# Four token blocks by fetched rows and six dense in the expert stage, with the low parts of u made by VectorE

## The reference, cut to what matters

```python
def peer(x, w_q, sub_keys, u, v):
    q = (xb @ w_q).reshape(tb, PEER_HEADS, 2, PEER_D_KEY // 2)
    s = jnp.einsum("thmd,mkd->thmk", q, sub_keys)
    s_top, i_top = lax.top_k(s, K)                    # K = 16, 8 heads
    ...
    best, pos = lax.top_k(cand, K)
    expert = jnp.take_along_axis(cand_idx, pos, axis=-1)
    gate = jax.nn.softmax(best, axis=-1)
    h = jax.nn.gelu(jnp.einsum("thkd,td->thk", u[expert], xb))
    w = gate * h
    return jnp.einsum("thk,thkd->td", w, v[expert])
```

## Time and profile before

| | us |
|---|---|
| median of 3 runs | 5527.01 (5522.74 to 5529.78) |
| span of the profiled execution | 5520.1 |
| experts stage in it (from its first load) | 3009.75 to 5520.1 |
| spread_gates in it, stores of the 7 blocks issued | 2752.8 to 2978.2 |

### The profile page before, as it was taken

The page is one execution under the profiler, slowest core; times in us unless marked ns, Lnnn a source line. Parts: engine busy times, 40 slices in busy tenths (PEclk is TensorE's granted clock), DMA queues, the critical chain, the costliest instruction groups (busy, mean ns, idle before and its releaser), DMA issues. The chain is left out here.

```text
span 5520.1 us, 71031 instructions
## 1 busy us (share of the span) xinstructions
PE 4860.9 (88%) x24196; PEld 3924.5 (71%) x24196; DVE 3732.9 (68%) x7021; ACT 1582.4 (29%) x2809; POOL 2631.3 (48%) x1877
## 2 busy tenths in 40 slices
PE   7999995554999799765396999999999999999999
PEld 6888884443444486554285788888888888888888
DVE  2000003786578422889896888888888888888887
ACT  3111101554667421111396222222222221222221
POOL 4122210553345110344574666666666666666664
PEclk9999997777899899887698999999999999999999
DMA  3222211001311342000187777677777767677676
GB/s 128 85 85 85 83 50 61 28 25 50 132 50 57 119 145 87 30 33 20 38 230 242 282 241 247 233 247 239 244 243 244 252 235 245 239 244 244 234 249 214
DMA packets 356695, 861.24 MB, mean 156 GB/s; under 512 B 27032, under 2 KB 169144, under 8 KB 356280
## 3 DMA queue, kind: packets, MB, share of 16 engines
q1 hardware_dynamic: 235872, 414.54, 23.4%
q0 software_dynamic: 119552, 440.88, 22.3%
q10 hardware_dynamic: 1152, 4.46, 0.2%
HBM read 733.33 MB, written 125.14 MB: 156 GB/s over the span
## 5 line engine op out<-in xcount | busy, mean ns | idle before, releaser
L2396 PE MATMUL e_ph<-e_x,e_u 128*128 128x512 f32 (+1 forms) x6144 | 1381.7, 363 | 50.9 <-DVE e_x L2461 50.9
L2396 PEld LDWEIGHTS e_ph<-e_x,e_u 128*128 128x128 f32 x6144 | 1128.7, 188 | 219.5 <-issue 42.0
L2418 PE MATMUL e_po<-e_v,e_w 128*128 128x512 f32 x4608 | 1185.6, 393 | 10.5 <-POOL e_v L2354 10.5
L2418 PEld LDWEIGHTS e_po<-e_v,e_w 128*128 128x128 f32 x4608 | 859.9, 188 | 161.1 <-POOL e_v L2354 10.8
L338 PE MATMUL proj_acc<-xn,w_tile 128*128 128x512 f32 (+1 forms) x3456 | 677.7, 358 | 4.5 <-POOL w_tile L368 4.5
L2311 ACT ACTIVATE e_act<-e_ph 128x512 f32<-128x512 f32 (+1 forms) x256 | 139.6, 545 | 1820.7 <-PE e_ph L2396 1820.7
L338 PEld LDWEIGHTS proj_acc<-xn,w_tile 128*128 128x128 f32 x3456 | 575.0, 188 | 107.0 <-POOL w_tile L368 4.7
L2493 DVE TENSOR_TENSOR e_acc<-e_acc,e_po 128x512 f32<-128x512 f32 x768 | 516.9, 680 | 172.5 <-PE e_po L2418 172.5
L2510 DVE SCALAR_TENSOR_TENSOR e_tok<-e_row,e_slot,e_tok 128x1024 f32<-128x1024 f32 x384 | 586.4, 1540 | 1.9 <-DMA e_tok<-h_tok_dram 1.9
L2349 POOL TENSOR_TENSOR e_u<-e_u_raw,e_u 128x1024 fp32r<-128x1024 f32 x128 | 380.1, 2969 | 424.7 <-ACT e_u L2294 424.7
L2499 DVE SCALAR_TENSOR_TENSOR e_row<-e_row,e_tok 128x1024 f32<-128x1024 f32 x384 | 572.8, 1498 | 4.4 <-DMA e_row<-in_u_rows,expert_tok 4.4
(11 more groups left out here) (312 smaller groups left out, 6880.1 us busy)
## 6 DMA issues: line engine op xcount, KB each, us to landing
e_u_raw<-in_u_exp SPq DMA_DIRECT2D x128, 512.0 KB, 4.0
e_v_raw<-in_v_exp SPq DMA_DIRECT2D x128, 512.0 KB, 3.5
gates_dram<-g_out SPq DMA_DIRECT2D x7, 8192.0 KB, 30.3
e_g<-gates_dram SPq DMA_DIRECT2D x128, 448.0 KB, 3.3
feat_dram<-proj_out POOLq DMA_DIRECT2D x50, 640.0 KB, 5.8
w_raw<-in_w_feat SPq DMA_DIRECT2D x50, 512.0 KB, 4.9
raw<-feat_dram SPq DMA_DIRECT2D x22, 640.0 KB, 6.0
mx_gate<-feat_dram SPq DMA_DIRECT2D x16, 640.0 KB, 4.0
```

The lines of the kernel that those rows point to most:

```text
L2396: ins = nc.tensor.matmul(ph[q % 2][:, 0:tn], u[b][j][:, kk, :], xs[m][:, kk, t0:t0 + tn], start=(i == 0), stop=(i == 3 * DC - 1))
L2418: ins = nc.tensor.matmul(out, w[b][j][:, blk * P:(blk + 1) * P], v[2 * odd + b][m][:, half * HALF:(half + 1) * HALF], start=(n == 0 and (f ...
```

## The change

GB goes from 3 to 4: four blocks by fetched rows (512 fetches of u and 512 of v), six dense (TD = 768). What follows from it:

- spread_gates makes six blocks of dense gates, an even number, so its ScalarE loop ends on the other output buffer.
- The spans are 384 and 384 tokens; the second product has 12 tiles a period, the ring of `po` is now numbered through two periods (`bank`), since 10 tiles a period do not divide by four.
- A period has 16 rows, in a ring of RB = 8 buffers.
- `rest_u` moves from GpSimd to VectorE: the low part of u for slab 1 stands after row 0 of the period in which it is used, that for slab 0 of the next period after row 13. GpSimd keeps `rest_v`, between the fetches.
- The three hand-written orders (TensorE's tables, VectorE's period, GpSimd's fetches) are written anew.

```diff
-GB = 3
+GB = 4
...
-    SPAN = ((0, 512), (512, TD - 512))
+    SPAN = ((0, TD // 2), (TD // 2, TD // 2))
...
-    HELD = 5
+    HELD = 4
...
-    NEAR = 8
-    RB = 6
+    NEAR = DB
+    RB = 2 * GB
...
+    bank = lambda t, odd: (RT * odd + ring(t)) % ORING
...
                 for p in range(PAIRS):
                     r0 = (2 * p + 1) * RB
-                    if p:
-                        rest_u(2 * p + 1)
-                        rest_v(2 * p)
                     for r in range(0, 3):
                         fetch(r0 + r)
+                    if p:
+                        rest_v(2 * p)
+                    for r in range(3, 7):
+                        fetch(r0 + r)
                     rest_v(2 * p + 1)
-                    for r in range(3, 10):
-                        fetch(r0 + r)
-                    if p + 1 < PAIRS:
-                        rest_u(2 * p + 2)
-                    for r in range(10, 12):
+                    for r in range(7, 16):
                         fetch(r0 + r)
...
-                    quarter(p, 0, odd, ((1, 7), (1, 8), (1, 9)), (4, 14, 6), first, last)
+                    quarter(p, 0, odd, ((1, 4), (1, 5), (1, 6)), (4, 10, 10), first, last)
...
+                def rest_u(k, b):
+
+                    dve.wait_ge(u_hi, k + 1)
+                    nc.vector.tensor_tensor(whole(u[b][1]), u_raw[:], whole(u[b][0]).bitcast(F32), ALU.subtract).then_inc(u_lo, 1)
...
-                    outputs(0, 0, 1)
                     if not last:
                         weights(p, 2)
-                    row_work(10)
+                    row_work(13)
                     if not last:
                         rest(p, 2)
-                    outputs(0, 2, 3)
-                    row_work(11)
-                    outputs(0, 4, 5)
+                    outputs(0, 0)
+                    if not last and more:
+                        rest_u(2 * p + 2, 0)
+                    row_work(14)
+                    outputs(0, 1)
+                    row_work(15)
+                    outputs(0, 2)
```

More of the change, by code:

```diff
@@ L2158, in block_of @@
                         keep(n * ROUNDS, b, 0, g)
-                assert ROUNDS % STAGES == 0 and DB % 2
+                assert ROUNDS % STAGES == 0 and DB % 2 == 0
                 for g in range(AHEAD):
@@ L2207, in experts @@
         po = [ps(f"e_po{q}", [P, HALF]) for q in range(ORING)]
-        landing = [t[:, 0:TD] for t in (g[0], g[1], *row[1:RB], act_h)]
+        landing = [t[:, 0:TD] for t in (g[0], g[1], *row[1:6], act_h)]
         assert len(landing) == DC
@@ L2411, in second_product @@
                     else:
-                        out = po[ring(t) % ORING][:]
+                        out = po[bank(t, odd)][:]
                         if not first or ring(t) >= ORING:
@@ L2520, in weigh_slots, with period @@
                     dve.wait_ge(slot_weighted, 1)
-                def period(p, first=False, second=False, blending=False, turning=False, last=False):
+                def period(p, odd, first=False, second=False, blending=False, turning=False, more=True, last=False):
                     def row_work(*rows):
@@ L2535, in outputs @@
                             if back and not first:
-                                add_output(p - 1, t, second)
+                                add_output(p - 1, t, 1 - odd, second)
                             elif not back and not last:
-                                add_output(p, t, first)
+                                add_output(p, t, odd, first)
                     if not first:
@@ L2551, in period @@
                         rest(p - 1, 3)
-                    outputs(1, 6)
+                    outputs(1, 3)
+                    if not first and not last:
+                        rest_u(2 * p + 1, 1)
                     row_work(1)
-                    outputs(1, 7)
+                    outputs(1, 4)
                     row_work(2)
-                    outputs(1, 8)
+                    outputs(1, 5)
+                    row_work(3)
                     if not last and not first:
                         weights(p, 0)
-                    row_work(3)
+                    row_work(4)
@@ new lines, in period @@
+                    if not last and more:
[4 more added lines that the diff above has]
+                    outputs(0, 2)
+                assert OT == 12 and 2 * RB == 16
+                period(0, 0, first=True)
+                period(1, 1, second=True)
+                with dve.Fori(1, TURN // 2) as i:
+                    for odd in range(2):
+                        period(2 * i + odd, odd)
@@ L2591, in _ @@
+                period(TURN, 0, blending=True, turning=True)
+                period(TURN + 1, 1, blending=True)
+                with dve.Fori(TURN // 2 + 1, PAIRS // 2 - 1) as i:
+                    for odd in range(2):
+                        period(2 * i + odd, odd, blending=True)
+                period(PAIRS - 2, 0, blending=True)
+                period(PAIRS - 1, 1, blending=True, more=False)
+                period(PAIRS, 0, last=True)
                 for half in range(2):
```

33 lines of the change are left out of this document (19 added, 14 removed).

## The result

The changed kernel takes 5533.03 us in the median of 20 runs (5528.65 to 5538.77), the kernel before 5525.27 us (5519.88 to 5529.78, 20 runs): ratio **1.0015, 95% interval 1.0008 to 1.0021**. That is 7.8 us longer, within the 0.2% that the prediction called no difference, where 5354 us was forecast. The bound did pass from TensorE to VectorE, but the gain was given back in a wait.

What follows compares the result with a forecast made beforehand. TensorE was taken as the bound, VectorE 12% behind and becoming the new one. Span 5520.1 - 37.6 (spread_gates) - 144 (periods) + 1 + 6 + 1.4 = 5346.9, with 6.9 to the median 5354 us; range 5215 to 5495.

Steps and rivals of the forecast that it cites:

- TensorE's new period: TensorE's matmuls in one period of the experts stage: 33.4 us, 5.1 us less a period if TensorE alone counted.
- VectorE's stream: VectorE's work in one period: 31.0 us plus 4.4 of collisions, 35.4 us, longer than TensorE's 33.4, so VectorE becomes the bound.
- The collisions: VectorE operations on two SBUF tiles wait while GpSimd subtracts for v: two a period, 2.2 us each, 1.6 at the lower end.
- The loop: Chain through single buffer u_raw: VectorE's subtraction, load of u, ScalarE's high parts, VectorE's rest; 36.1 us with dots, 36.4 with blends.
- the wait ahead of the fourth rest: Sign: VectorE's idle time, if any, stands before the fourth quarter's rest, behind ScalarE's high part of w, which awaits u's load.
- the landing of u: Time for the DMA load of u to arrive among the row fetches: taken as 4.5 us, upper end 5.6.
- The other links: The loop without the landing: VectorE 30.0 us, semaphore to SyncE 0.2, ScalarE's high parts 0.95 and 0.51; 31.6 us with dots.
- The gain of the period is eaten: Rival: u lands in 6.5 to 7.4 us, loop 38.2 to 39.1, time 5477 to 5534 us; chance 0.06.
- slower: Rival: a landing of u_raw over 7.4 us makes the loop pass 39.2 us, time above 5538 us; chance 0.11.
- The turn from dots to blends: VectorE waits there for the reload of the tokens, now as the bound and with 2 MB: +6 us, 0 to +12.
- Where TensorE stands and what it waits for: TensorE stands 2 to 3 us a period, before a quarter of slab 0 (e_u) or tile t = 0 (e_w), awaiting VectorE.
- the clock would not fall: TensorE's clock: stands of 2.8 us a period counted as no fall; a fall every stand would give about 36.4 us.

Runs made afterwards that it cites:

- e4_all_low_vector: e1_u_early with the subtractions for v on VectorE too, so that GpSimd only fetches: 5187.38 us, ratio 0.9385 to the kernel before.
- e1_u_early: The changed kernel with VectorE's subtraction for slab 0 behind row 9 and SyncE loading u ahead of the gates: 5322.16 us, ratio 0.9633 to the kernel before.
- e2_half_rows: The changed kernel with every second row fetch left out, each fetched row serving two dots or blends, so sums are wrong: 5415.6 us.
- e7_before_u_on_vector: The kernel before with both subtractions for u on VectorE, behind row 0 and behind row 10: 5526.8 us, ratio 1.0.

## Why the prediction was wrong

**TensorE's new period, 33.4 us: right** as a length of work; e4_all_low_vector runs at 33.5 us with dots, with TensorE full.

**VectorE's stream, 35.4 us: right to 0.6 us.** In the changed kernel with dots it is 39.45 less 3.3 of idleness (60.0 us in 18 periods), 36.1; in e1_u_early, where it is the bound, the period is 36.0 with dots and 35.4 with blends. The subtraction for u took 1.21 on VectorE, as taken from the earlier trace rows. The collisions were two a period, and cost 2.76 - 0.55 = 2.2 and 3.36 - 0.55 = 2.8 us where I had 2.2 each, which is the 0.6:

```profile
4001.94 2.76 DVE L2460 TENSOR_TENSOR e_act<-e_act,e_g 128x384 f32<-128x384 f32 x1
...
4011.20 3.36 DVE L2460 TENSOR_TENSOR e_act<-e_act,e_g 128x384 f32<-128x384 f32 x1
```

**The loop: right as a mechanism, and the wait ahead of the fourth rest stood where the prediction had put it. The step that failed is the landing of u, a term of the sum, taken as 4.5 us: it was 7.0 in the mean (6.4 to 7.6).** The other links were 30.0 us of VectorE, 0.2 to SyncE, 0.95 and 0.51 on ScalarE; measured were 30.6, 0.33, 0.97 and 0.54. With dots the period came out at 39.45 where 36.1 was forecast, 3.35 more: 2.5 of it is the landing, 0.6 the second collision, 0.2 the small links. With blends it was 38.9 for 36.4, and the landing makes all of the 2.5. Nor did the upper end that I gave it, 5.6 plus 0.7, reach 7.0. Where the reasoning went astray is in the text. I had seen that rows 7 to 13, a load of v and one of g ask for 390 GB/s in the 12 us before the load (4.6 MB in 12 us is 383), close to what the DMA engines give. I still took the price of a load in thinner traffic, raised by 0.2 us over one row. The window of the load shows engines that are full, 0.99 at 357 GB/s, and e2_half_rows shows what the half of the fetches costs that it leaves out: 2.3 us of landing in the mean. With them gone the landing was 4.7 us, near the 4.5 of the forecast, and the time 5415.6, 62 us above the forecast.

**The rival named it.** "The gain of the period is eaten" had the landing at 6.5 to 7.4 and the time at 5477 to 5534, "slower" the same mechanism above 7.4. They were given 0.17 together. The range ended at 5495 and so cut the first of them in two. A better upper bound for the unknown cost was at hand: 7.5 us, the longest landing of a fetched row, on another queue but beside the same traffic, stood in the trace and in my text.

**Outside the period.** Period 1 began 66.8 us into the stage for 66.6 before, +0.2 where +1 was forecast, because period 0 is shorter by about as much as TensorE's wait for v grew (10.5 to 16.7 us). The turn from dots to blends took a period of 47.9 us, 8.7 more than its neighbours, for +6:

```profile
4278.93 1.29 DVE L2500 SCALAR_TENSOR_TENSOR e_tok<-e_row,e_slot,e_tok 128x1024 f32<-128x1024 f32 x1 [6.01 <-DMA e_tok<-h_tok_dram]
```

The end took +1.4, as forecast. spread_gates: six stores, 37.6 us apart as before. The row answers to the earlier trace rows:

```profile
L2065 SPq DMA_DIRECT2D gates_dram<-g_out x6: 372/381/424, 2757.3 to 2945.2; - x6
```

Its gain was not quite whole, because that stage began 5.2 us later than before (2710.1 for 2704.9). The delay arose ahead of it, and it is no cost of the change as far as the traces tell: e7_before_u_on_vector, with the three blocks of the kernel before, enters the stage at 2708.4, and the other kernels with four blocks at 2706.1 to 2711.2. The sum of the measured terms: 5520.1 + 5.2 - 37.6 - 0.6 (spread_gates sends its first block 47.2 us after it begins, for 47.9 before) + 0.2 + 46.6 (63 periods and the turn) + 1.4 = 5535.3, the span.

**Where TensorE stands and what it waits for** was as forecast: with dots it waits for the second quarter's rest ahead of the tile t = 0. With blends it waits for GpSimd's low part of v as well (54.4 us in 22 waits between 4400 and 5300). That the clock would not fall was wrong. After a stand of 3.27 us the tile takes 2.92 us instead of 1.55, and the eight matmuls behind it 2.76:

```profile
4016.30 2.92 PE L2403 MATMUL e_po<-e_v,e_w 128*128 128x512 f32 x6 [3.27 <-DVE e_w L2467]
...
4019.02 2.76 PE L2381 MATMUL e_ph<-e_x,e_u 128*128 128x384 f32 x8
```

```profile
4013.05:4016.30 3.25, 0.00 (x0) 0.01 (x1) 3.25 (x5) 1.71 (x3) 2.50 (x3) 0.88 0.71 238
4016.30:4022.00 5.70, 5.70 (x15) 5.03 (x16) 5.70 (x11) 0.14 (x1) 3.98 (x4) 0.50 0.89 314
```

So after a much shorter stand than the 10.5 us of the earlier trace rows TensorE works at a granted clock of 0.50, 1.2 GHz, for 5.7 us. Between 3500 and 4060 there are 14 such stretches, of 3 to 7 us, in all but one of the periods, and the granted clock over the dots is 0.95. The row agrees with what the Trainium skill, "TensorE: Matmul & The Clock Gate", Part 1, says of a clock that falls with idleness and rises with activity, where I had set it aside. The slow clock cost nothing here, since TensorE's tiles still came before VectorE wanted them: VectorE waited for ScalarE's w alone, 60.0 us in 18 periods.

## What to carry to other kernels

When work moves to another engine, follow the buffers that it frees, not only its own time: the subtraction cost 1.13 us on VectorE as worked out, but the next load waits for it. A single buffer whose load, conversion and use come round once a period is a loop of its own, to be summed link by link beside the engines' streams. Price a transfer in such a loop by the traffic that the new kernel puts around it; where the trace of before has that load only in thinner traffic, the longest landing of any transfer there is the least that the range has to reach. In a queue that one engine issues in order, a step that moves ahead of another also moves that other back, and what stands in the queue between them decides when the load starts.

## What the runs showed of the hardware

A load gets longer while the DMA engines are full on average for only 0.81 of the time. 0.5 MB landed in 3.8 us in the median beside 241 GB/s, in 7.0 in the mean at the place that counts beside 286, and in 4.5 in the median beside 194. The average share did not tell of it; the share during the load did, 0.99 against 0.67 with half of the fetches left out. And it is harmless where nothing waits: in e4_all_low_vector the traffic is 333 GB/s, a load of u lands in 6.2 us in the median, and halving the fetches changes the time by no more than the scatter.

A subtraction of 128x1024 took 2.4 to 2.8 us on GpSimd with dots, and stretched the operation on two SBUF tiles that VectorE had beside it from 0.55 to 2.76 and 3.36 us. On VectorE itself it takes 1.13 us of the stream. Taking the two for v off GpSimd as well gained 135 us (e4_all_low_vector against e1_u_early).
